# TensorE multiplies constants between the modulation groups, and loads go ahead of rotary stores

## The chip, the cores and the metric

The program runs on one core of one Trainium2 chip. The metric is the device time of one execution in microseconds (us); lower is better. The engines are TensorE (PE in the profile; PEld is its weight load), VectorE (DVE), ScalarE (ACT), GpSimd (POOL) and SyncE (SP), which here issues nearly all DMAs. SPq is the profile's name for SP's DMA queue.

## The reference

One step of a backbone with four layers over 256 context and 1024 latent tokens, model width 1024. Layers 0 and 3 mix tokens by multi-head latent attention (MLA), layer 1 by grouped-query attention, layer 2 by a banded one. Each layer is, cut to what matters here:

```python
sh, sc, gt = adaln(c, w_ada[i], b_ada[i])   # split(silu(c) @ w + b, 3)
h = rms_norm(x, norm_g[i]) * (1.0 + sc) + sh
z = h @ w_in                                # MLA: q, kv, rotary key, gate
q = rms_norm(cq, q_norm) @ w_uq             # 16 heads x (64 plain + 32 rotary)
kn, v = ckv_all @ w_ukv                     # keys and values of all tokens
o = softmax(q k^T) v
x = x + gt * ((o * silu(gate)) @ w_out[i])
```

The MLA layers rotate the 32 rotary features of each latent token's q by its grid position. Matrices are multiplied as pairs of float16 (a high part and a low part), three products each: high by high, high by low, low by high.

## The kernel before

Tokens lie along the free axis, features along the 128 partitions: `x_T` is 8 tiles of 128 features by 1280 tokens. Tokens go in three chunks of 512, 512 and 256 (`TOK_CHUNKS`). The program is a row of blocks, one after the other; all five engines meet between two blocks.

**The first block**, `start` (L176), makes the modulated input of layer 0. SP loads x, four small constants, then the modulation's weights in eight groups of 1.57 MB (`in_w_ada`, L238) into three slots: the load of group g, from 3 on, waits until TensorE has used up group g-3 (`s_row` has reached g-2). Behind group 5 go the first two weight tiles of the next block (`next_load`), behind group 7 the cache of layer 0. TensorE adds up the squares of x over partitions with a matrix of ones (L325, three float32 multiplications), then per group `group(g)` (L308, eight multiplications of a 32-column silu(c) with 384 weights each, float32), and `across(g)` (L296), which folds and transposes the row that VectorE has copied (`take_row`, L365). VectorE makes 1/rms by ScalarE's first value and Newton's three steps (L398 to L402), multiplies half of x by it (`times_rstd`, L369), and when groups 0 to 5 are through, finishes shift and scale (L413, L417; the second raises `s_fin`). From then on ScalarE and VectorE work through 24 parts n (chunk by feature tile): `product(n)` (L140), ScalarE's high part (L279 to L284), `low(n)` (L383, L385). `next_hi` and `next_low` (L780, L393) split the two weight tiles of the next block. `begin(t, c)` (L313, L320) is the first 2 x 2 tiles by chunks of the next block's product, 24 multiplications each, and waits part by part for `low`. At the end ScalarE and VectorE split the cache (L287, L437), SP stores four pieces of it (L245) and waits for them.

**The next block**, `project` (L801), starts with 48 multiplications of 256 columns that need nothing new, then with weights that SP loads at its start.

**The block `middle`** (L1301), once in layer 0 and once in layer 3, makes queries, keys and values in turns, one tile t a turn: 4 rotary tiles, 8 plain ones (turns 4 to 11), the first key tile (12), 14 value tiles, 7 more key tiles. Its weights come in pieces (`in_mla_uq`, `in_mla_uk`, `in_mla_uv`) through four landing buffers; the loads of turn t are split by ScalarE (L1490) and VectorE (L1542) at the start of turn t+2, and each may be issued when VectorE has split the piece that lay in its buffer, which it does at turn t. A tile's result is evicted by ScalarE (L1519) and VectorE (L1562); TensorE has three pairs of banks, so its unit u waits for the eviction of unit u-3. A tile has two units, of 1024 and of 256 columns (768 for a key tile). After turns 4 and 7 the rotated parts are stored: `turns_out = {4: 0, 7: 1}`, four stores of 8 heads x 16 rows x 1280 (L1409) each time, against four of 64 x 1280 for a plain tile (L1414). SP's order in a turn is: the turn's loads, its tile's stores, its rotary stores. Results lie in five slots (`wait_slot`), which the stores must have left before they are written again: the tile of turn 10 takes the slot of the first rotary part of turn 7, that of turn 11 the second's.

## Time and profile before

| | us |
|---|---|
| median of 3 runs | 4034.32 (4027.93 to 4036.26) |
| the profiled execution | 4037.71 |
| its span, first to last instruction | 4035.9 |
| TensorE busy with matmuls | 3893.6 (96% of the span) |
| VectorE, ScalarE, GpSimd busy | 2665.9, 2332.7, 1132.1 |
| mean granted TensorE clock | 0.988 |

The shares say that TensorE is the bound nearly everywhere. TensorE's clock has two levels, 1.2 and 2.4 GHz; the profile gives the granted level of a stretch as 0.50 or 1.00, and a stretch with both as a mean. Two parts of the program have something else in them: the first 80 us, where TensorE has little to do and waits, and the turns 8 to 12 of `middle`, around 285 to 320 us (layer 0) and 3167 to 3202 us (layer 3).

### The profile page before, as it was taken

The page shows a single profiled execution, that of the slowest core. Times are in us where ns is not written, and L with a number is a line of the kernel's source. Part 1 is how long each engine was busy: PE and PEld are TensorE (multiplying, and loading weights), DVE is VectorE, ACT ScalarE, POOL GpSimd, SP SyncE. Part 2 cuts the span into 40 slices and gives each one's busy share as a digit, 9 for nine tenths or more (in the row PEclk, how much of TensorE's full clock was granted, in tenths as well). Part 3 has the DMA queues.
Part 4 walks back from the last instruction along what each step waited for, and adds up shares of the span by engine and source line. Part 5 has one row for each costly group of instructions (what it writes and reads, how often), then busy time and mean ns, then how long its engine had stood idle before and what let it go on. Part 6 is the DMA issues. An engine that isn't in the chain of part 4 may idle for free. (4 is left out here: it accounts for less than half of the span.)

```text
span 4035.9 us, 57984 instructions
## 1 busy us (share of the span) xinstructions
PE 3893.6 (96%) x20892; PEld 1931.6 (48%) x20892; DVE 2665.9 (66%) x3536; ACT 2332.7 (58%) x3099; POOL 1132.1 (28%) x831
## 2 busy tenths in 40 slices
PE   6999999999999999999999999999999999999998
PEld 3554444444455544444445554555455444444444
DVE  6345777777457478888845427888543568777754
ACT  4433777777444358787843217888333457777762
POOL 0000343434230024454521003444210014444442
PEclk8999999999999999999999999999999999999999
DMA  6237323232102342222111324332111652212111
GB/s 241 65 102 223 92 55 77 60 72 64 60 32 76 116 113 51 65 64 62 37 66 51 108 91 117 91 90 63 62 46 70 186 151 46 55 42 55 42 38 66
DMA packets 376225, 329.42 MB, mean 82 GB/s; under 512 B 247664, under 2 KB 295344, under 8 KB 374480
## 3 DMA queue, kind: packets, MB, share of 16 engines
q1 hardware_dynamic: 376016, 326.60, 29.0%
q8 instruction: 135, 2.21, 0.2%
q14 instruction: 74, 0.61, 0.0%
HBM read 235.30 MB, written 91.23 MB: 81 GB/s over the span
## 5 line engine op out<-in xcount | busy, mean ns | idle before, releaser
L796 PE MATMUL bank<-H_hilo,w_hilo 128*128 128x512 f16 (+1 forms) x5760 | 1046.1, 344 | 13.6 <-DVE w_hilo L1046 10.1
L2238 ACT ACTIVATE p_f<-bank 128x1024 f32<-128x1024 f32 (+2 forms) x768 | 742.1, 966 | 485.9 <-PE bank L2184 454.6
L2184 PE MATMUL bank<-q_slots,k_slots 96*128 96x512 f16 (+7 forms) x3968 | 939.8, 366 | 6.0 <-PEq L1197 3.6
L1992 DVE TENSOR_REDUCE max_parts<-bank 128x1 f32<-128x512 f32 (+1 forms) x1248 | 799.1, 663 | 206.0 <-PE bank L1931 199.7
L2305 DVE TENSOR_TENSOR p_lo<-p_f,p_hi 128x1024 f16<-128x1024 f32 (+2 forms) x624 | 750.9, 1206 | 156.2 <-ACT p_hi L2242 151.6
L796 PEld LDWEIGHTS bank<-H_hilo,w_hilo 128*128 128x128 f16 x5760 | 563.7, 98 | 495.8 <-DVE w_hilo L1046 11.1
L2242 ACT ACTIVATE p_hi<-bank 128x1024 f16<-128x1024 f32 (+2 forms) x768 | 739.1, 962 | 0.0
L2184 PEld LDWEIGHTS bank<-q_slots,k_slots 96*128 96x128 f16 (+2 forms) x3968 | 369.7, 98 | 396.8 <-issue 27.0
L1931 PE MATMUL bank<-k_slots,q_slots 96*128 96x512 f16 (+4 forms) x1392 | 474.6, 369 | 24.9 <-DVE max_parts L1992 20.8
L2371 POOL TENSOR_TENSOR p_lo<-p_f,p_hi 128x1024 f16<-128x1024 f32 x144 | 315.6, 2192 | 567.5 <-ACT p_hi L2242 544.1
L2353 POOL TENSOR_TENSOR o_gated<-o_f,gate_rows 64x512 f32<-64x512 f32 (+1 forms) x192 | 235.5, 1226 | 778.5 <-DVE o_f L2285 571.5
L1010 ACT ACTIVATE z_ring<-bank 128x512 f32<-128x512 f32 (+1 forms) x192 | 87.5, 528 | 430.7 <-PE bank L796 417.2
L2151 PE MATMUL bank<-p_hi,cq_hilo 128*128 128x512 f16 (+1 forms) x832 | 308.5, 371 | 2.4 <-DVE p_lo L2305 1.8
L2155 PE MATMUL bank<-p_lo,cq_hilo 128*128 128x512 f16 (+1 forms) x832 | 307.9, 370 | 0.0
L2153 PE MATMUL bank<-p_hi,cq_hilo 128*128 128x512 f16 (+1 forms) x832 | 307.7, 370 | 0.0
L2151 PE MATMUL bank<-p_hi,v_hi_ones 128*128 128x512 f16 (+2 forms) x736 | 256.2, 350 | 21.9 <-DVE o_f L2285 14.9
L2153 PE MATMUL bank<-p_hi,v_lo_zeros 128*128 128x512 f16 (+2 forms) x736 | 257.3, 350 | 0.0
L2155 PE MATMUL bank<-p_lo,v_hi_ones 128*128 128x512 f16 (+2 forms) x736 | 255.8, 350 | 0.0
L1931 PEld LDWEIGHTS bank<-k_slots,q_slots 96*128 96x128 f16 (+1 forms) x1392 | 136.4, 98 | 231.2 <-DVE max_parts L1992 84.4
L1046 DVE SCALAR_TENSOR_TENSOR w_hilo<-w_f,w_hilo 128x1024 f16<-128x1024 f32 x56 | 68.6, 1224 | 258.8 <-ACT w_hilo L965 258.3
L2359 POOL TENSOR_TENSOR H_hilo<-o_gated,H_hilo 64x512 f16<-64x512 f32 (+3 forms) x192 | 218.0, 1136 | 22.9 <-POOL H_hilo L2357 13.3
L2357 POOL CAST H_hilo<-o_gated 64x512 f16<-64x512 f32 (+3 forms) x192 | 218.8, 1140 | 20.0 <-POOL o_gated L2353 12.3
(203 smaller groups left out, 3963.1 us busy)
## 6 DMA issues: line engine op xcount, KB each, us to landing
ada_w<-in_w_ada SPq DMA_DIRECT2D x48, 768.0 KB, 5.4
gate<-z_ring SPq DMA_DIRECT2D x32, 640.0 KB, 3.3
gate_rows<-gate SPq DMA_DIRECT2D x64, 320.0 KB, 4.0
q_slots<-q_mla SPq DMA_DIRECT2D x64, 240.0 KB, 3.2
k_mla<-H_hilo SPq DMA_DIRECT2D x64, 224.0 KB, 3.2
k_slots<-k_mla SPq DMA_DIRECT2D x64, 224.0 KB, 4.4
cq_hilo<-v_scratch SPq DMA_DIRECT2D x64, 224.0 KB, 3.3
w_f<-in_mla_in SPq DMA_DIRECT2D x24, 512.0 KB, 4.0
```

The source lines that it names most:

```text
L796: ins = pe.matmul(dst, lhs(a, k), rhs(b, k), start=(k == 0 and n == 0), stop=(k == nk - 1 and n == 2))
L1931: ins = pe.matmul(mb[:, 0:n], Q[0:kk, q_slot(hd, b), 0, q0:q0 + P], K[0:kk, k_slot(hd, b), 0, k0:k0 + n], start=True, stop=True)
L1992: dve.tensor_reduce(mx[:, par, t, c:c + 1], MB[(b * NE + k) % 2][:, 0:n], AX.X, ALU.max).then_inc(s_red.h, 1)
L2151: pe.matmul(d, V[:, b, kt], ph[:, slot[q], sel], start=first and n == 0, stop=False, skip_group_check=True)
L2153: pe.matmul(d, VL[:, b, kt], ph[:, slot[q], sel], start=False, stop=False, skip_group_check=True)
L2155: ins = pe.matmul(d, V[:, b, kt], pl[:, slot[q], sel], start=False, stop=fin, skip_group_check=True)
L2184: ins = pe.matmul(dst, lhs, rhs, start=(m == 0), stop=(m == len(ops) - 1), skip_group_check=swa)
L2238: act.activation(p32[:, p % 2, 0:cols], src, ACT.Exp, scale=scale).then_inc(s_p32.h, 1)
L2242: act.activation(ph[:, slot[p], 0:cols], src, ACT.Exp, scale=scale).then_inc(s_ph.h, 1)
L2305: dve.tensor_tensor(pl[:, slot[q], 0:cols], p32[:, q % 2, 0:cols], ph[:, slot[q], 0:cols], ALU.subtract).then_inc(s_pl.h, 1)
L2353: pool.tensor_tensor(og[rows, 0:nq], o32[rows, s, 0:nq], G[rows, q0:q0 + nq], ALU.mult).then_inc(s_og.h, 1)
L2371: pool.tensor_tensor(pl[:, slot[p], 0:cols], p32[:, p % 2, 0:cols], ph[:, slot[p], 0:cols], ALU.subtract).then_inc(s_pp.h, 1)
```

## The change

Three edits. In `start`, TensorE gets `keep_busy(n)`: n multiplications of a constant 128 x 128 float16 matrix with 512 columns of the constants, into a bank that a later product overwrites from its start. Ten stand ahead of group 0, five behind group 0, and five each behind groups 2 to 5 (behind the `across` that follows them, or ahead of the last one), and behind group 6. Group 0 moves ahead of the three sums of squares, group 7 into the middle of `begin(0, 0)`, `across(6)` behind it and `across(7)` behind `begin(1, 0)`. VectorE's two `next_low` go ahead of the finish of shift and scale, and its last two `take_row` move to n = 1 and n = 8. In `middle`, the rotary stores go from the end of turns 4 and 7 to turns 5 and 8, between the loads and the tile's stores.

```diff
+        busy, BUSY = self.c16[:, 0:4].rearrange("p j m -> p (j m)"), 5
+                def keep_busy(n):
+                    for _ in range(n):
+                        pe.matmul(flat[1][:, 0:4 * P], self.c16[:, 0], busy, start=True, stop=True)
+                def begin(t, c, k0=0, k1=KD):
+                    for k in range(k0, k1):
                 pe.wait_ge(s_in.h, s_in.base + 16 * len(consts))
+                pe.wait_ge(s_sc.h, s_sc.base + 2)
+                pe.wait_ge(s_c16.h, s_c16.base + 5)
+                keep_busy(2 * BUSY)
+                group(0)
+                keep_busy(BUSY)
                 pe.wait_ge(s_ss.h, s_ss.base + KD - 1)
...
+                for g in range(1, READY):
                     group(g)
-                    if g > 0:
-                        across(g - 1)
+                    across(g - 1)
+                    if g > 1:
+                        keep_busy(BUSY)
                 across(READY - 1)
-                for g in range(READY, KD):
-                    group(g)
+                group(READY)
+                keep_busy(BUSY)
                 pe.wait_ge(s_v.h, s_v.base + NC)
-                begin(0, 0)
-                for g in range(READY, KD):
-                    across(g)
+                begin(0, 0, 0, 5)
+                group(READY + 1)
+                across(READY)
+                begin(0, 0, 5, KD)
                 begin(1, 0)
+                across(READY + 1)
...
                 take_row(5)
+                next_low(0)
+                next_low(1)
...
-                next_low(0)
...
-                    if n == KD - 1:
-                        next_low(1)
-                    if n in (3, 7):
-                        take_row(READY + n // 4)
+                    if n in (1, KD):
+                        take_row(READY + n // KD)
...
+                    if t - 1 in turns_out:
+                        for item in (2 * turns_out[t - 1], 2 * turns_out[t - 1] + 1):
+                            sp.wait_ge(s_rl.h, s_rl.base + item + 1)
+                            store_item(sp, item)
                     if t in item_of:
                         sp.wait_ge(s_lo.h, s_lo.base + lows_of[t])
                         store_item(sp, item_of[t])
-                    if t in turns_out:
-                        for item in (2 * turns_out[t], 2 * turns_out[t] + 1):
-                            sp.wait_ge(s_rl.h, s_rl.base + item + 1)
-                            store_item(sp, item)
```

TensorE's program at the start of the first block, before:

```order
L325 MATMUL bank<-H_hilo,ones 128x512 x2
L325 MATMUL bank<-H_hilo,ones 128x256
L308 MATMUL bank<-ada_w,silu_c_wide 32x384 x16
L296 MATMUL bank<-fold_strips,ada_rows 128x2 x3
L308 MATMUL bank<-H_hilo,silu_c_wide 32x384 x8
```

And in the changed kernel:

```order
L317 MATMUL bank<-const_f 128x512 x10
L309 MATMUL bank<-ada_w,silu_c_wide 32x384 x8
L317 MATMUL bank<-const_f 128x512 x5
L336 MATMUL bank<-H_hilo,ones 128x512 x2
L336 MATMUL bank<-H_hilo,ones 128x256
L309 MATMUL bank<-ada_w,silu_c_wide 32x384 x8
L297 MATMUL bank<-fold_strips,ada_rows 128x2 x3
L309 MATMUL bank<-H_hilo,silu_c_wide 32x384 x8
L297 MATMUL bank<-fold_strips,ada_rows 128x2 x3
L317 MATMUL bank<-const_f 128x512 x5
```

The first group of weights now stands ahead of the sums of squares, with 15 multiplications of constants around it.

SP's DMAs of `middle` in turns 4 to 8, before (`w_f` is the landing buffer of the weights, `q_mla` the store of queries; the stores of 8x16x1280 are the rotary ones):

```order
L1414 DMA q_mla<-H_hilo 64x1280 x4
L1409 DMA q_mla<-H_hilo 8x16x1280 x4
L1442 DMA w_f_4<-in_mla_uq 128x384
L1442 DMA w_f_4<-in_mla_uv 128x2x128
L1414 DMA q_mla<-H_hilo 64x1280 x4
L1442 DMA w_f_4<-in_mla_uq 128x384
L1442 DMA w_f_4<-in_mla_uv 128x2x128
L1414 DMA q_mla<-H_hilo 64x1280 x4
L1442 DMA w_f_4<-in_mla_uk 128x256
L1442 DMA w_f_4<-in_mla_uv 128x2x128
L1414 DMA q_mla<-H_hilo 64x1280 x4
L1409 DMA q_mla<-H_hilo 8x16x1280 x4
```

And in the changed kernel:

```order
L1425 DMA q_mla<-H_hilo 64x1280 x4
L1453 DMA w_f_4<-in_mla_uq 128x384
L1453 DMA w_f_4<-in_mla_uv 128x2x128
L1420 DMA q_mla<-H_hilo 8x16x1280 x4
L1425 DMA q_mla<-H_hilo 64x1280 x4
L1453 DMA w_f_4<-in_mla_uq 128x384
L1453 DMA w_f_4<-in_mla_uv 128x2x128
L1425 DMA q_mla<-H_hilo 64x1280 x4
L1453 DMA w_f_4<-in_mla_uk 128x256
L1453 DMA w_f_4<-in_mla_uv 128x2x128
L1425 DMA q_mla<-H_hilo 64x1280 x4
```

The four rotary stores have moved behind two loads and stay ahead of the next tile's stores; it is the same again in turn 8 and in layer 3.

## Rows read from the trace of the kernel before

**Rows 1.** Busy time by stretch: start:end, length, busy (xinstructions) by engine, PEclk, DMA share, GB/s.
```profile
34.40:58.20 23.80, 20.03 (x107) 8.60 (x108) 16.84 (x23) 9.25 (x13) 0.00 (x0) 0.50 0.95 384
38.30:42.40 4.10, 4.10 (x23) 1.96 (x23) 3.36 (x3) 0.00 (x0) 0.00 (x0) 0.50 0.97 406
```

**Rows 2.** Timeline of the first block: start, length, engine, line, work [idle before <-releaser].
```profile
22.57 4.60 PE L325 MATMUL bank<-H_hilo,ones 128*128 128x512 f32 x6 [22.57 <-DVE H_hilo L358]
27.10 2.96 PE L308 MATMUL bank<-ada_w,silu_c_wide 128*32 128x384 f32 x32
...
39.60 2.79 PE L308 MATMUL bank<-ada_w,silu_c_wide 128*32 128x384 f32 x16
...
64.22 15.70 PE L320 MATMUL bank<-H_hilo,first_w_hilo 128*128 128x512 f16 x72
```

**Rows 3.** The same sum of squares in the next block, from TensorE's timeline.
```profile
129.25 2.31 PE L1142 MATMUL bank<-squares,ones 128*128 128x512 f32 x6
```

**Rows 4.** Busy time by stretch, as rows 1, where the DMA engines run dry, and after.
```profile
27.70:32.00 4.30, 4.30 (x54) 1.81 (x46) 2.42 (x3) 2.54 (x2) 0.00 (x0) 1.00 0.47 157
32.00:50.00 18.00, 14.70 (x82) 7.87 (x78) 11.11 (x13) 2.00 (x2) 0.00 (x0) 0.56 1.02 426
```

**Rows 5.** Timeline of VectorE, ScalarE and SP in the first block.
```profile
28.84 1.62 SPq L238 DMA_DIRECT2D ada_w<-in_w_ada  x2
...
30.61 1.48 DVE L398 TENSOR_TENSOR H_hilo<-rstd 128x1280 f32<-128x1280 f32 x1
...
46.70 2.00 ACT L780 ACTIVATE first_w_hilo<-next_w_f 128x1024 f16<-128x1024 f32 x2 [16.41 <-DMA next_w_f<-in_mla_in]
...
49.89 0.18 DVE L417 SCALAR_TENSOR_TENSOR ada<-ada,params 128x16 f32<-128x16 f32 x1
...
61.24 1.22 DVE L393 SCALAR_TENSOR_TENSOR first_w_hilo<-next_w_f,first_w_hilo 128x1024 f16<-128x1024 f32 x1
62.37 0.55 DVE L365 COPY ada_rows<-bank 128x384 f32<-128x384 f32 x1
...
64.40 0.72 ACT L284 ACTIVATE H_hilo<-xn,ada 128x512 f16<-128x512 f32 x1 [1.21 <-DVE xn L140]
...
74.38 1.05 ACT L287 ACTIVATE ckv_hilo<-ckv_f 128x1024 f16<-128x1024 f32 x1
```

**Rows 6.** TensorE's timeline at the start of the block project.
```profile
81.14 5.40 PE L796 MATMUL bank<-H_hilo,first_w_hilo 128*128 128x256 f16 x48 [1.22 <-PEq L226]
...
88.63 11.56 PE L796 MATMUL bank<-H_hilo,w_hilo 128*128 128x512 f16 x45 [2.08 <-DVE w_hilo L1046]
```

**Rows 7.** Busy time by stretch, as rows 1: project, and middle of layer 0.
```profile
89.00:92.30 3.30, 3.30 (x10) 1.18 (x8) 3.29 (x3) 1.79 (x3) 0.00 (x0) 0.50 0.83 304
314.30:317.60 3.30, 3.30 (x12) 1.46 (x10) 2.20 (x4) 1.32 (x3) 2.38 (x2) 0.50 0.82 256
```

**Rows 8.** Timeline of middle in layer 0, turns 4 to 11, all engines that matter there.
```profile
280.50 4.33 SPq L1409 DMA_DIRECT2D q_mla<-H_hilo  x4
283.64 0.55 DVE L1542 SCALAR_TENSOR_TENSOR w_hilo<-w_f,w_hilo 128x384 f16<-128x384 f32 x1
284.88 1.48 SPq L1442 DMA_DIRECT2D w_f<-in_mla_uq  x1
...
302.97 1.82 SPq L1442 DMA_DIRECT2D w_f<-in_mla_uk  x1
...
309.75 0.59 SPq L1442 DMA_DIRECT2D w_f<-in_mla_uk  x1
310.54 0.42 ACT L1490 ACTIVATE w_hilo<-w_f 128x256 f16<-128x256 f32 x1 [8.03 <-DMA w_f<-in_mla_uk]
...
312.89 0.42 ACT L1490 ACTIVATE w_hilo<-w_f 128x256 f16<-128x256 f32 x1 [0.35 <-DMA w_f<-in_mla_uk]
313.58 1.51 PE L796 MATMUL bank<-cq_hilo,w_hilo 128*128 128x256 f16 x9 [2.74 <-DVE H_hilo L1562]
```

**Rows 9.** The same wait of TensorE in layer 3.
```profile
3194.92 1.99 PE L796 MATMUL bank<-cq_hilo,w_hilo 128*128 128x256 f16 x9 [2.33 <-DVE H_hilo L1562]
```

More of the change, by code:

```diff
@@ L311, in group @@
                     ins.then_inc(s_row.h, 1)
-                def begin(t, c):
+                def keep_busy(n):
+                    for _ in range(n):
+                        pe.matmul(flat[1][:, 0:4 * P], self.c16[:, 0], busy, start=True, stop=True)
+                def begin(t, c, k0=0, k1=KD):
                     pe.wait_ge(s_nl.h, s_nl.base + t + 1)
                     t0, n = TOK_CHUNKS[c]
-                    for k in range(KD):
+                    for k in range(k0, k1):
                         pe.wait_ge(s_hl.h, s_hl.base + c * KD + k + 1)
@@ L325, in _ @@
                     pe.matmul(sums[c][:, 0:n], self.ones[:], ss[:, t0:t0 + n], start=True, stop=True).then_inc(s_sum.h, 1)
-                pe.wait_ge(s_sc.h, s_sc.base + 2)
-                pe.wait_ge(s_c16.h, s_c16.base + 5)
-                for g in range(READY):
+                for g in range(1, READY):
                     group(g)
-                    if g > 0:
-                        across(g - 1)
+                    across(g - 1)
+                    if g > 1:
+                        keep_busy(BUSY)
                 across(READY - 1)
-                for g in range(READY, KD):
-                    group(g)
+                group(READY)
+                keep_busy(BUSY)
                 pe.wait_ge(s_v.h, s_v.base + NC)
-                begin(0, 0)
-                for g in range(READY, KD):
-                    across(g)
+                begin(0, 0, 0, 5)
+                group(READY + 1)
+                across(READY)
+                begin(0, 0, 5, KD)
                 begin(1, 0)
+                across(READY + 1)
                 begin(0, 1)
```

## The prediction

> **What bounds the kernel now.** The page's first section shows TensorE busy for 96% of the span. So I looked for stretches where it waits for something that the change touches. Busy time by stretch shows two kinds: the first 80 us, with the clock at half from 34.4 to 58.2 [rows 1], and short half-clock stretches behind waits in project and in middle [rows 7]. The timelines then say what ends each wait.
>
> In the first block, shift and scale are ready at 50.07 (L417's end) [rows 5]; from there ScalarE and VectorE work through 24 parts until ScalarE turns to the cache at 74.38 [rows 5]. The next block begins 6.8 us later, with TensorE at 81.14 [rows 6]; TensorE itself had ended at 64.22 + 15.70 = 79.92 [rows 2]. So the end is set by the parts, the cache's split and its stores, and TensorE is 1.2 us early. Its half clock has cover here, and that is the first thing to hold against the bursts.
>
> What sets the 50.07? The two weight tiles of the next block land at 46.70 and are split behind it [rows 5]. They are late since the DMA engines run dry: 157 GB/s over the 4.3 us from 27.7, against 426 after 32.0 [rows 4]. That loses 4.3 x (1 - 157/426) = 2.7 us. Load 3 waits there for group 0, which stands behind the sums of squares; it is issued at 28.84 [rows 5].
>
> In middle, TensorE stands still for 2.74 us at 310.84, layer 3 for 2.33 [rows 8, 9], and its clock is at half after it, 3.3 us and more, worth another 1.7 [rows 7]. ScalarE had waited 8.03 us for a key weight that SP issued at 302.97, behind four rotary stores [rows 8].
>
> **The first block, step by step.** The ten multiplications wait for constants alone, which are there long before any group, and no data waits for them: they cost nothing. The DMA engines have delivered groups 0 to 2 at 27.7; a group of 1.57 MB takes 1.57/426 = 3.7 us, so group 0 is through at 20.3 and lands, with an estimated 1.2 for completion, at 21.5. Group 0 at half clock takes 2.79 [rows 2]. Five constants: a 512-column product at full clock takes 15.70/72 = 0.218 [rows 2], at half 0.44, so 2.2. The sums could have begun at 22.57 and now begin near 26.5. They took 4.60; the same sum takes 2.31 later, at full clock [rows 2, 3]. Between the two I take 2.7, since the clock comes to full some way into them: they end at 29.2 instead of 27.2, **+2.0** for 1/rms. Newton begins at 32.6 instead of 30.61 [rows 5].
>
> VectorE from there to the finish: three steps and four products by 1/rms at 1.48, four `take_row` at 0.55, both `next_low` at 1.22 [rows 5] = 10.4 + 2.2 + 2.4 = 15.0, so 47.6 at the earliest.
>
> The DMAs: load 3 is issued at 24.3 instead of 28.84 and closes the first part of the hole. Load 4 waits for group 1, now at 29.2 + 1.5 = 30.7, half of the pair that takes 2.96 [rows 2], and comes through some 0.9 us late. So 1.8 of the 2.7 are gained: the weight tiles are there at 44.9, ScalarE's two splits (2.00) end at 46.9, the second `next_low` at 48.1, the finish at 48.6: **-1.5**. The bursts behind groups 2 to 5 are 1.1 each at full clock, and group, `across` (an estimated 0.4; no row here has it alone) and burst are then 1.5 + 0.4 + 1.1 = 3.0 against 3.7 between landings: hidden. If the finish no longer waited for the weight tiles, the burst ahead of `across(5)` would show with its 1.1.
>
> Behind the finish one idle stretch of ScalarE goes: 1.21, ended by a product that stood behind `next_low(1)` and a `take_row` [rows 5]. **-1.2**. The two `take_row` stay, but VectorE now has no `next_low` of 1.22 behind its first products either, and this room takes them. TensorE needs 96 x 0.218 + 1.5 + 0.8 = 23.2 from about 51.0, so it ends at 74.2 or a little later, still ahead of the parts and the cache. The block ends at 81.1 - 2.7 = 78.4. Bounds: -4.6 (all 2.7 regained and sums as fast as before) to +1.2 (the clock never comes, below).
>
> **Project.** TensorE's wait ahead of its first product grows from 1.22 [rows 6] to some 3 us. Now its clock falls behind the second wait, of 2.08, and 3.3 us at half [rows 7] cost 1.7. If it falls before the first 48 products, they take up to 7.1 instead of 5.40, and end within the 7.5 us from 81.14 to 88.63 [rows 6]; then the second fall has no reason. Between 0 and -1.7 I take **-1.0**, nearer to the gain, since a wait of 2.08 was enough for a fall.
>
> **The bursts and the clock.** The stretch at 38.3 has TensorE busy for 4.10 of 4.10 us with groups and `across`, at 0.50 [rows 1]: these products did not bring the clock back. The page "TensorE: Matmul & The Clock Gate" of the Trainium skill (Part 1) says that activity releases the throttle, judged by how busy the engine is; by that rule alone the groups would have done it, and the bursts would be needless. The row disagrees. By the rule the block would come out as in my sum, since the bursts hide either way.
>
> **Middle.** Turn 8's loads now go ahead of the rotary stores and are there in time; but turn 5's loads also do, and they can't be issued before VectorE's splits of turn 5 at 283.64 and behind it [rows 8], since VectorE is busy with the rotary parts until then. The rotary stores were issued at 280.50, in that very wait [rows 8]. Now SP stands idle behind a blocked load from 280.5 to 284.1, and the stores start at 285.0 instead of 280.5. SP's 32 issues between 280.50 and 309.75, the first and last of its rows, stand without a gap over 0.3 us [rows 8], so the lag runs on: of 4.5 us, 1.2 is two loads already issued, and some 0.6 I take as slack. **2.7 us** stays at the loads of turn 9, behind both lots of rotary stores and turn 8's own. ScalarE gets them at 312.89 now [rows 8] and would at 315.6. These are its splits at the start of turn 11, behind which the eviction stands for which TensorE's second unit of turn 12 waits.
>
> TensorE's path: without the wait of 2.74 the unit of 313.58 starts at 310.0, the next at 310.9 and ends at 313.5; then TensorE waits for that eviction until 318.8. Before, it began this same unit at about 318.7, having lost 2.7 and 1.7 on the way. The gain of turn 10 is eaten whole. The clock then falls after a wait of 5.3, and costs up to 1.7 again: I take **+1.3** a layer, +2.6 for both. Bounds: -4.4 a layer (both waits gone, 2.7 and 1.7), +3.6 (the whole idle stretch of SP arrives).
>
> The page "DMA: Bandwidth & Descriptors" of the Trainium skill (Queues, rings and completion order) says that a DMA's data is spread over the largest number of engines up to 16 that divides its slowest dimension, which for 8 x 16 x 1280 would be 8 of 16. The trace has such a thing: the load behind these stores was being issued for 1.48 and 1.82 us, another for 0.59 [rows 8]. By the page the stores' slow drain moves with them and isn't shortened; my sum has it so.
>
> **Sum.** -2.7 - 1.0 + 2.6 = -1.1: the profiled execution of 4037.7 becomes 4036.6. The median of before is 3.4 below its profiled execution, so I forecast **4033.2**. A measurement of this kernel can tell about 0.2%, 8.1 us, from no change.
>
> **Rivals.**
> - *Middle's wait goes* (0.16). If turn 9's loads aren't late, because SP catches up by turn 7 as it does now, both layers give 4.4; with -3.6 at the start and -1.7 in project that is -14: 4020. For it: SP's issues of loads shrink to 0.59 when nothing clogs. Against: the 3.6 idle us of SP are certain by VectorE's row.
> - *The bursts don't bring the clock* (0.12). Group, `across` and burst at half take 2.8 + 0.7 + 2.2 = 5.7 against 3.7 per landing, and are the block's path: the finish comes near 52.5, +2.4; with -1.2 and middle's +2.6, +3.8: 4038. Against: full-width products brought the clock back in every other stage.
> - *Slower* (0.08). The lag of SP arrives whole: the rotary stores hold the slots of turns 10 and 11 until after 308 and 313, evictions wait for them, and TensorE loses 3.6 + 1.7 a layer beyond now; +10.6 - 2 = +8.6: 4043. It decides when VectorE's split of turn 5 comes more than 3 us after the stores could go, and nothing behind absorbs it.
> - *Nothing arrives* (0.14). The weight tiles land as late as before and TensorE's waits only move: 4034.
>
> My forecast has 0.50. The range leaves out most of the first rival and the far part of the third: 4023 to 4041. Chances: faster by over 0.2% (below 4026) 0.18; slower (above 4042) 0.08; within, 0.74.
>
> **What would show it.** The clock full from before 30 to the end of the first block; the DMA engines without a hole at 27.7; shift and scale at 48.6; the next block at 78.4. In middle: SP waiting ahead of the load of turn 5, ScalarE's long wait of turn 10 gone and one of 2 to 3 us at turn 11, TensorE's wait moved from 310.8 to 313 less 3.7. I'm wrong on middle if TensorE has no wait over 2 us there, and on the start if the block's end moves by less than 1 or over 5 us.

## The result, and the profile after

| | before | after |
|---|---|---|
| median | 4035.01 us (4027.93 to 4041.74, 20 runs) | 4040.59 us (4034.75 to 4048.26, 20 runs) |
| ratio, 95% interval | | 1.0014, 1.0008 to 1.002 |
| the profiled execution | 4037.71 us | 4036.22 us |

The kernel became 5.6 us slower. That is less than the 0.2% that the prediction took as the bound of its three cases, but the interval of this comparison lies wholly above 1, and the sign is not the forecast's. One run of the kernel before, of 4134.8 us at a mean clock of 0.942, is left out of all comparisons. The profiled execution of after is one of its faster ones and that of before one of its slower ones, so the two traces alone would tell a wrong story (-1.5 us). They are read here place by place, and sizes are taken from several traces.

The head of the page of after:

```profile
span 4034.4 us, 58064 instructions
PE 3896.1 (97%) x20932; PEld 1931.6 (48%) x20932; DVE 2668.0 (66%) x3536; ACT 2333.9 (58%) x3099; POOL 1135.4 (28%) x831
```

In `start`, first the timeline, then busy time by stretch (columns as in rows 1) over the stretch of [rows 4] in which the DMA engines had run dry, and over a later stretch:

```profile
21.39 2.79 PE L309 MATMUL bank<-ada_w,silu_c_wide 128*32 128x384 f32 x16 [7.96 <-DMA ada_w<-in_w_ada]
...
26.22 2.39 PE L336 MATMUL bank<-H_hilo,ones 128*128 128x512 f32 x6
...
43.99 2.00 ACT L791 ACTIVATE first_w_hilo<-next_w_f 128x1024 f16<-128x1024 f32 x2 [12.11 <-DMA next_w_f<-in_mla_in]
...
47.57 0.17 DVE L431 SCALAR_TENSOR_TENSOR ada<-ada,params 128x16 f32<-128x16 f32 x1
```

```profile
27.70:32.00 4.30, 4.30 (x42) 1.85 (x40) 0.65 (x2) 4.00 (x5) 0.00 (x0) 1.00 0.98 409
46.90:53.60 6.70, 5.90 (x24) 1.78 (x25) 6.37 (x12) 4.97 (x8) 0.00 (x0) 0.50 0.99 373
```

The hole in the DMA stream is closed (409 GB/s for 157), the weight tiles are there at 43.99 instead of 46.70 [rows 5], and shift and scale are ready at 47.74 instead of 50.07. Project, from TensorE's timeline, answers to [rows 6]:

```profile
77.12 5.40 PE L807 MATMUL bank<-H_hilo,first_w_hilo 128*128 128x256 f16 x48 [0.34 <-PEq L227]
85.75 14.44 PE L807 MATMUL bank<-H_hilo,w_hilo 128*128 128x512 f16 x78 [3.23 <-DVE w_hilo L1057]
```

It begins 4.0 us earlier, but after its first 48 products TensorE waits 3.23 us for 2.08, so that only 2.9 are left at 85.75.

Middle of layer 0, timeline of SP, ScalarE and TensorE, answers to [rows 8]. The whole stands 4.6 us earlier here:

```profile
273.43 2.47 SPq L1425 DMA_DIRECT2D q_mla<-H_hilo  x4
279.66 0.34 SPq L1453 DMA_DIRECT2D w_f<-in_mla_uq  x1
280.05 0.60 SPq L1453 DMA_DIRECT2D w_f<-in_mla_uv  x1
280.69 4.37 SPq L1420 DMA_DIRECT2D q_mla<-H_hilo  x4
...
298.64 12.57 PE L807 MATMUL bank<-cq_hilo,w_hilo 128*128 128x256 f16 x63 [2.30 <-DVE H_hilo L1573]
...
306.90 1.30 ACT L1530 ACTIVATE H_hilo<-bank 128x1024 f16<-128x1024 f32 x2 [4.16 <-DMA q_mla<-H_hilo]
...
312.71 0.42 ACT L1501 ACTIVATE w_hilo<-w_f 128x256 f16<-128x256 f32 x1 [4.51 <-DMA w_f<-in_mla_uk]
...
315.79 3.36 PE L807 MATMUL bank<-ckv_hilo,w_hilo 128*128 128x512 f16 x12 [1.98 <-DVE H_hilo L1573]
```

SP has issued a tile's stores at 275.90 and then stands idle to 279.66, where VectorE frees a landing buffer (it ends a split at 279.63). Only then come the rotary stores. In the kernel before they filled just this gap [rows 8]. The one wait of TensorE of 2.74 us [rows 8] has become two, of 2.30 and 1.98, and each has a stretch of 3.4 us at half clock behind it (299.44 to 302.85 and 316.50 to 319.92 in the clock's record), where before had one. In layer 3 the one wait of 2.33 us [rows 9] has become three, but the clock falls once, as before (3190.52 to 3193.94):

```profile
3177.51 9.91 PE L807 MATMUL bank<-cq_hilo,w_hilo 128*128 128x256 f16 x54 [1.03 <-DVE H_hilo L1573]
3189.37 1.16 PE L807 MATMUL bank<-cq_hilo,w_hilo 128*128 128x256 f16 x9 [1.95 <-DVE H_hilo L1573]
...
3196.61 2.12 PE L807 MATMUL bank<-ckv_hilo,w_hilo 128*128 128x512 f16 x12 [1.80 <-DVE H_hilo L1573]
```

### The profile page after: what moved, and what is told of

Same layout as the page of the kernel before. It is cut to its first block and busy times, and to the rows that moved or that the text cites. A ratio compares the mean times of both kernels' runs of the same rounds, so it can differ in the third digit from the quotient of the medians.

```text
span 4034.4 us, 58064 instructions
## 1 busy us (share of the span) xinstructions
PE 3896.1 (97%) x20932; PEld 1931.6 (48%) x20932; DVE 2668.0 (66%) x3536; ACT 2333.9 (58%) x3099; POOL 1135.4 (28%) x831
```

## How the sizes are taken

All kernels of this study end in the same matmuls. So the n-th matmul from the end of a trace can be set against the n-th from the end of the trace of before: the difference of their starts is how late (+) or early (-) TensorE is there. This table, worked out so, holds one profiled execution each. "Start and project" is the difference at the end of project, "middle" what it grows by over the block; between the two and behind layer 3 the kernels are the same, and that part scatters by some us from one execution to the next. `start_only` and the other names are the experiments below.

```
                    start+project  middle, layer 0  middle, layer 3    end
before, as timed         0.00            -                -             0.00
middle_only             -1.66          +3.12            +3.28          +4.91
turn8_only              -1.45          -2.22            -0.06          -4.17
turn5_only              +0.29          +3.55            +6.17          +9.54
six_before              -1.65          -3.82            -2.74          -6.45
after                   -4.56          +3.19            +3.38          -1.47
start_only              -3.12          +0.18            +0.70          -6.70
start_turn8             -1.77          -1.14            -0.38          -5.77
six_after               -2.27          +1.47            +1.19          +1.90
start_thin_burst        -2.48          -1.93            +1.56          -6.73
start_no_burst          -6.05          -0.03            +0.39          -4.66
after_no_burst          -4.20          +2.80            +3.49          -1.02
six_start_no_burst      -5.77          -3.65            -0.20         -11.98
six_turn8_no_burst      -3.98          -2.69            -0.19         -11.42
```

The trace of before has one of the slower first blocks: the five executions that have the old block `start` stand at 0, -1.66, -1.45, +0.29 and -1.65, mean -0.9. The five that have the new one with its added products (after, start_only, start_turn8, six_after, start_thin_burst) have a mean of -2.8. The change's 4.6 us at this point are thus nearer to 2 in the mean.

The times, with the mean and its standard error. Medians are compared with runs of the kernel before on the same chip, which gives the ratio. Differences of means in the text are taken from 4035.4, the mean of before over four sets of runs (4035.2, 4035.0, 4035.7 and 4035.7), so that the choice of set moves them by up to 0.4:

| kernel | median us (range, runs) | mean | ratio, 95% interval |
|---|---|---|---|
| before, all four sets | 4035.2 (4027.9 to 4042.0, 115) | 4035.4 +/- 0.2 | |
| after | 4040.59 (4034.75 to 4048.26, 20) | 4041.2 +/- 0.8 | 1.0014 (1.0008 to 1.002) |
| start_only | 4035.46 (4028.09 to 4039.89, 11) | 4034.6 +/- 1.1 | 1.0 (0.9991 to 1.0009) |
| middle_only | 4043.36 (4041.4 to 4046.07, 11) | 4044.0 +/- 0.6 | 1.0021 (1.0012 to 1.003) |
| turn8_only | 4033.63 (4028.71 to 4035.81, 11) | 4033.1 +/- 0.6 | 0.9995 (0.9986 to 1.0004) |
| start_turn8 | 4035.18 (4027.46 to 4039.34, 11) | 4034.7 +/- 1.0 | 0.9999 (0.999 to 1.0008) |
| turn5_only | 4044.24 (4038.53 to 4047.24, 11) | 4043.7 +/- 0.8 | 1.0019 (1.001 to 1.0028) |
| six_after | 4039.61 (4033.38 to 4044.69, 11) | 4038.4 +/- 1.2 | 1.0009 (1.0 to 1.0018) |
| six_before | 4030.58 (4027.92 to 4034.53, 11) | 4030.7 +/- 0.6 | 0.9987 (0.9978 to 0.9996) |
| start_no_burst | 4030.28 (4026.67 to 4036.31, 11) | 4030.6 +/- 0.9 | 0.9988 (0.9979 to 0.9997) |
| start_thin_burst | 4033.93 (4028.78 to 4038.04, 11) | 4033.7 +/- 0.9 | 0.9994 (0.9985 to 1.0003) |
| after_no_burst | 4038.42 (4036.01 to 4041.02, 11) | 4038.5 +/- 0.5 | 1.0007 (0.9998 to 1.0016) |
| six_start_no_burst | 4026.69 (4023.07 to 4028.88, 8) | 4026.1 +/- 0.8 | 0.9976 (0.9965 to 0.9986) |
| six_turn8_no_burst | 4026.88 (4024.64 to 4030.53, 11) | 4027.4 +/- 0.5 | 0.9981 (0.9972 to 0.999) |

## Experiments: the change in halves

**start_only** is after with the order of stores in `middle` put back:

```diff
-                    if t - 1 in turns_out:
-                        for item in (2 * turns_out[t - 1], 2 * turns_out[t - 1] + 1):
-                            ...
                     if t in item_of:
                         ...
+                    if t in turns_out:
+                        for item in (2 * turns_out[t], 2 * turns_out[t] + 1):
+                            ...
```

> The changed kernel with middle's rotary stores put back to the end of turns 4 and 7. Theory A (the first block gives 4.6 us and keeps it, middle's new order takes over 3 us a layer): 4.6 us faster than before, about 4030, with TensorE level with the changed kernel up to middle and 3 us ahead of it behind middle of layer 0. Theory B (the bursts or the first block's new order cost something later, the stores' place doesn't matter): no faster than before, 4036 to 4041, TensorE's lead of 4.6 us lost somewhere else than in middle.

**middle_only** is the kernel before with that edit alone, the other way round.

> The kernel before with the rotary stores moved to turns 5 and 8, the first block untouched. Theory A: 3.2 us more in each of the two middles, 6 to 7 us slower, about 4041; TensorE's wait of 2.74 us in turn 11 gone and new ones in turns 8 to 9 and 12. Theory B: within 1 us of before, 4035.

Measured: the start's edits alone give a mean of 4034.6, which can't be told from before; the middle's alone 4044.0, +8.6. So the whole loss comes from moving eight stores per layer, and the start brings next to nothing. In middle_only's trace the two middles cost 3.1 and 3.3 us, the same as in after. That is 6.4 of the 8.6; where the rest lies is not shown. Of the theories, A is right on the stores; the 4.6 us that it gave to the start did not arrive, as B had said.

## Experiments: which of the two moves in middle

Both lots of rotary stores moved by a turn. **turn8_only** moves only the later lot, from turn 7 to turn 8:

```diff
+                    if t - 1 in turns_out and turns_out[t - 1] in (1,):
+                        ...the two rotary items, as in the change
                     if t in item_of:
                         ...
-                    if t in turns_out:
+                    if t in turns_out and turns_out[t] not in (1,):
```

> The kernel before with only the second lot of rotary stores (turn 7) moved behind the loads of turn 8; the first lot stays at the end of turn 4. Theory A (SP stood idle ahead of turn 5's blocked loads, and that lag is what costs): no idle time of SP at turn 5, loads of turn 8 there in time, TensorE's wait of 2.74 us and the half clock behind it smaller or gone, 0 to 3 us a layer faster than before, about 4032. A rival to A (the drain of the rotary stores costs wherever they stand, because turn 10 needs their slot back): slower than before by 2 us a layer or more, with ScalarE waiting for the stores of queries in turn 10.

**turn5_only** has (0,) in place of (1,): the earlier lot goes from turn 4 to turn 5, the later stays.

> The kernel before with only the first lot of rotary stores (turn 4) moved behind the loads of turn 5. Theory A (SP idles behind turn 5's blocked loads and everything on its queue comes late from there): the whole loss of middle_only and some more, since turn 8's loads still stand behind the second lot: 7 to 10 us slower than before, about 4044, with about 4 us of SP's idle time at turn 5 and ScalarE's wait for turn 8's loads longer than the 8.03 us of before. Rival (the second lot and its slots cost): within 1 us of before.

**start_turn8** is start_only with the later lot moved.

> The changed kernel's first block with only the second lot of rotary stores moved. Theory A: the sum of start_only and turn8_only, 5 to 10 us faster than before, 4025 to 4030. Theory B: no faster than before.

Measured: turn5_only costs 8.3 (4043.7), as much as both moves. turn8_only has a mean 2.3 lower (4033.1; 1.9 against the runs on its own chip), but the interval of its ratio includes no change; on top of the start's edits the same move gives nothing (4034.7 and 4034.6), so the sum that theory A expected of start_turn8 failed. The timeline of turn5_only, SP, ScalarE, and TensorE:

```profile
278.28 2.48 SPq L1414 DMA_DIRECT2D q_mla<-H_hilo  x4
284.51 0.34 SPq L1442 DMA_DIRECT2D w_f<-in_mla_uq  x1
284.90 0.60 SPq L1442 DMA_DIRECT2D w_f<-in_mla_uv  x1
285.54 4.34 SPq L1409 DMA_DIRECT2D q_mla<-H_hilo  x4
...
295.33 0.59 SPq L1442 DMA_DIRECT2D w_f<-in_mla_uq  x1
...
302.05 9.91 PE L796 MATMUL bank<-cq_hilo,w_hilo 128*128 128x256 f16 x54 [0.85 <-DVE H_hilo L1566]
...
314.18 0.42 ACT L1494 ACTIVATE w_hilo<-w_f 128x256 f16<-128x256 f32 x1 [9.96 <-DMA w_f<-in_mla_uk]
...
317.20 2.10 PE L796 MATMUL bank<-cq_hilo,w_hilo 128*128 128x256 f16 x9 [5.25 <-DVE H_hilo L1566]
```

The gap from 280.76 to 284.51 is empty; the rotary stores start 5.0 us later than in [rows 8], of which 0.3 is the whole trace's. The load at 295.33, turn 6's, stands at 290.79 in the trace of before: 4.5 less 0.3 = 4.2 late, one turn after the move. Turn 8's (307.16 for 302.97) is 3.9 late and turn 9's (313.49 for 309.75) 3.4. ScalarE's long wait of 8.03 [rows 8] has grown to 9.96 and TensorE's of 2.74 to 5.25, with another of 0.85. 5.25 + 0.85 - 2.74 = 3.4 of the 3.55 us that this middle costs. SP's queue has hardly a gap in between and gives back 0.8 of the 4.2 us in three turns: it is the queue that paces these turns. In layer 3 the same move costs 6.17, with waits of 1.33 and 6.23 us for one of 2.33, and one execution doesn't tell whether that is typical.

turn8_only shows what the other move does:

```profile
305.75 1.30 ACT L1523 ACTIVATE H_hilo<-bank 128x1024 f16<-128x1024 f32 x2 [4.07 <-DMA q_mla<-H_hilo]
...
314.36 2.12 PE L796 MATMUL bank<-ckv_hilo,w_hilo 128*128 128x512 f16 x12 [1.39 <-DVE H_hilo L1566]
```

Turn 10's key weight is now early (split at 300.97, 310.54 before), but ScalarE waits 4.07 us for a store to leave a slot of `H_hilo`, and TensorE still waits 1.39. Loads and stores of one queue trade places, and what goes behind is late. This wait of 1.39 us has no half-clock stretch behind it, and layer 0 comes out 2.2 us shorter; in layer 3 nothing is gained.

## Experiments: more landing buffers

If the queue paces the turns because a load may only be issued when its buffer is free, then more buffers let SP run ahead. **six_after** and **six_before** have six landing buffers for four in `middle`, the two new ones in an unused tail of `H_hilo`, on the order of stores of after and of before:

```diff
-        SLOTS, DEPTH_W, LANDING, BATCH = 5, 4, 4, 5
+        SLOTS, DEPTH_W, LANDING, BATCH = 5, 4, 6, 5
-        wf = sb("w_f32", [P, LANDING, QK_, P], F32)
+        own_wf = sb("w_f32", [P, 4, QK_, P], F32)
+        spare = self.H[:].rearrange("p s k n -> p (s k n)")[:, SLOTS * 2 * KEYS:].bitcast(F32)
+        lands = [own_wf[:, b] for b in range(4)] + [...two pieces of spare...]
```

> The changed kernel with six landing buffers for middle's weights instead of four (two in the unused tail of the tile H_hilo), so that each load is issued three turns ahead of its split instead of two; the order of stores is that of the changed kernel. Theory A (late loads): TensorE's waits of 2.30 us (turn 9) and 1.98 us (turn 12) go, 3 to 7 us a layer faster than the changed kernel, about 4030. Rival S (the slots that rotary stores hold make ScalarE wait in turns 7 and 10, and that is what TensorE waits for): waits for stores stay and it is no more than 2 us faster than the changed kernel, about 4039.

> The kernel before with six landing buffers. Theory A: ScalarE's wait of 8.03 us in turn 10 goes, with TensorE's 2.74 us and the half clock behind it: 3 to 4.4 us a layer, 6 to 9 us faster than before, about 4027. Rival S: no faster than before.

Measured: -4.7 on the order of before (4030.7), -2.8 +/- 1.4 on that of after (4038.4). six_before's TensorE has no wait of note between 284 and 321:

```profile
284.07 26.10 PE L796 MATMUL bank<-cq_hilo,w_hilo 128*128 128x256 f16 x144 [0.68 <-DVE H_hilo L1565]
```

The wait of 2.74 and the half clock behind it are gone, -3.8 us in layer 0 and -4.2 up to the end of middle's turns in layer 3 (-4.71 at 3166, -8.89 at 3203 in the table's terms; 1.5 of them are given back behind it). In six_after ScalarE waits elsewhere:

```profile
309.46 1.30 ACT L1533 ACTIVATE H_hilo<-bank 128x1024 f16<-128x1024 f32 x2 [7.59 <-DMA q_mla<-H_hilo]
...
311.80 1.66 PE L807 MATMUL bank<-cq_hilo,w_hilo 128*128 128x256 f16 x9 [3.16 <-DVE H_hilo L1576]
```

With the loads early, the late stores themselves hold the slots: 7.59 us for ScalarE and 3.16 for TensorE, as rival S had it for this order; on the order of before, theory A holds. So the lag that the move at turn 5 starts seems to show at whichever of the two, loads or slots, runs out first. Of the two orders with six buffers, the difference is 7.7 us (4038.4 and 4030.7), with the start's edits on the slower side.

## Experiments: what the bursts cost

**start_no_burst** is start_only with an empty `keep_busy`; all other edits of the start, group 0 ahead of the sums among them, stay:

```diff
-                    for _ in range(n):
+                    for _ in range(0):
```

> start_only without the multiplications of constants: the first block's new order alone. Theory C (the bursts pay): the clock is at half from the sums or soon after until the first product, shift and scale come 1 to 3 us later than in start_only, 1 to 2 us slower than it. Theory D (the bursts only move instruction loading into the next block's first weight loads, and these lose 1.2 us there): the next block's first weights land 4.2 us after their issue instead of 5.4, and the whole is level with start_only or up to 1.5 us faster, 4033.

Measured: a mean of 4030.6, against 4034.6 with the bursts and 4035.4 before. The bursts cost 3.9 +/- 1.4 us, and that is most of the 4.8 that the rest of the start's edits gain; theory D had the direction and at most 1.5 us. Its timeline, and busy time by stretch:

```profile
47.24 0.17 DVE L431 SCALAR_TENSOR_TENSOR ada<-ada,params 128x16 f32<-128x16 f32 x1
...
76.78 5.40 PE L807 MATMUL bank<-H_hilo,first_w_hilo 128*128 128x256 f16 x48 [1.26 <-PEq L227]
84.27 15.95 PE L807 MATMUL bank<-H_hilo,w_hilo 128*128 128x512 f16 x85 [2.08 <-DVE w_hilo L1057]
```

```profile
27.00:41.40 14.40, 8.95 (x92) 4.63 (x88) 11.89 (x11) 2.90 (x3) 0.00 (x0) 1.00 1.01 420
41.60:51.70 10.10, 8.94 (x48) 4.00 (x38) 7.22 (x12) 5.41 (x8) 0.00 (x0) 0.50 1.01 400
```

The clock is full from 24.5 to 41.5 without a burst, and falls later; with the bursts it falls too, from 46.85 to 53.68 (the second stretch of after above). The finish is at 47.41 with no burst and 47.74 with them. So at the finish the bursts bring nothing: the clock there is hidden in the new order, as the DMA stream paces the groups at 420 GB/s. What they cost stands in project. Without them TensorE resumes at 84.27, with them at 85.75. The DMA view of 77 to 83 us, of after (the GB/s are those of 40 slices of 0.15 us):

```profile
GB/s 0 0 0 0 0 0 0 218 191 82 191 355 273 218 137 300 300 355 355 519 382 382 410 410 355 437 382 382 191 27 55 27 27 27 27 27 27 0 27 0
q8 instruction: 1, 0.02, 1.0%
w_f<-in_mla_in SPq DMA_DIRECT2D x2, 512.0 KB, 5.4
```

and of start_no_burst, from 76 to 82, so that it holds the same two loads:

```profile
GB/s 0 0 0 0 0 0 0 0 0 0 0 218 82 137 246 273 328 218 218 355 355 328 410 437 437 437 437 437 437 437 300 219 109 55 55 27 0 0 0 0
q1 hardware_dynamic: 288, 1.05, 51.1%
w_f<-in_mla_in SPq DMA_DIRECT2D x2, 512.0 KB, 4.2
```

The row of q8 is a block of instructions that is loaded by DMA. After has 136 of them in all, before and start_no_burst 135. In after the third falls between 78 and 81 us, right behind the first loads of project; in start_no_burst it comes between 84 and 87, and in before one comes between 63 and 66, the next between 90 and 93. The first two weight loads of project, issued in the same 3 us, land after 5.4 us (median of the two) instead of 4.2, which is also what they take in the trace of before. The slices show how: in after the stream stops at 81.4 but for some 27 GB/s, which is one packet of 4 KB per slice, until 82.9, where in start_no_burst it fades out over some five slices.

That could be the number of instructions, or what the wide products do. **start_thin_burst** keeps all 40 products and their 40 weight loads, but 8 columns wide:

```diff
-                        pe.matmul(flat[1][:, 0:4 * P], self.c16[:, 0], busy, start=True, stop=True)
+                        pe.matmul(flat[1][:, 0:8], self.c16[:, 0], busy[:, 0:8], start=True, stop=True)
```

> The start's edits with all 40 products of the bursts left as instructions, but 8 columns wide in place of 512, so that they keep TensorE busy for next to nothing. The full bursts gave a mean of 4034.6, no bursts 4030.6. Theory L, the added instructions cost (a block of code is loaded behind them, into project's first weight loads): the finish stays as it is, project resumes near 85.7 with a wait over 3 us in place of 84.27 with 2.08, a row of q8 stands in the first 6 us of project, and the mean is 4032 to 4035. Theory C, the bursts' work costs (it moves the stretches at half clock, which then fall into project): the resume stands at 84.3, no q8 row there, and the mean is 4030 to 4032. If both cost, the resume is 85.7, no stretch at half clock lies in project and the mean is 4032 to 4033.

Measured: a mean of 4033.7, 3.0 +/- 1.2 above no bursts and not to be told from the full ones. Project in its timeline, and the DMA view of 77 to 83:

```profile
86.14 14.06 PE L807 MATMUL bank<-H_hilo,w_hilo 128*128 128x512 f16 x65 [3.88 <-DVE w_hilo L1057]
```

```profile
q8 instruction: 1, 0.02, 1.0%
w_f<-in_mla_in SPq DMA_DIRECT2D x2, 512.0 KB, 5.3
```

The late resume and the row of q8 are there with products that keep TensorE busy for next to nothing: it is the instructions that cost; whether their work costs besides is not excluded (0.9 +/- 1.4 us between the two). Over all 14 traces the split is clean. The five with added products have a q8 row in the first 6 us of project, a median of 5.3 to 5.5 us for the first two loads, and a resume at 85.6 to 86.4. The nine without have no such row, a median of 4.1 to 4.4 us, and, of these, the four with the new start resume at 84.3 to 84.7. That is 1.5 us in the mean. In all 14 TensorE resumes 2.47 us after the second load has landed, so it is this landing that sets the resume. The page "Runtime: NRT & Kernel Launch" of the Trainium skill (Instruction fetch mechanics) says that instructions come in blocks of 256 by the sequencer's own DMA queue, ahead of their use and mostly hidden; the blocks are there in the trace, 0.02 MB each, and hidden they were not. How the block delays the weights can be seen in part. Its packet takes 0.96 us (1.0% of 16 engines' 6 us). The two loads are 256 packets of 4 KB, 16 for each of the 16 DMA engines if they are spread evenly. In all five traces with the q8 row the last eight or nine of them end one at a time, 1.1 to 1.9 us behind all others; in the nine without, at most three do. That fits one engine that was held up while the other 15 were not. The trace doesn't say which engine took which packet, so that it was the one with the block is inferred. The rest of what the bursts cost is partly clock: the longer wait was followed by a half-clock stretch in four of the five traces with added products, and in two of four without. One such stretch of start_only, by busy time:

```profile
85.50:88.80 3.30, 3.16 (x8) 1.17 (x9) 3.27 (x4) 2.14 (x4) 0.00 (x0) 0.50 0.86 315
```

Four and two of a handful are too few to price that part. At the end of project the traces with added products stand at a mean of -2.8 and the four without at -5.0, so 2.2 us of the 3 to 4 are found there, 1.5 of them at the resume. That another number of products would place the block elsewhere and cost nothing was not tried.

**after_no_burst** is the whole change with an empty `keep_busy`.

> The whole change without the products of the bursts. If the parts add up: the change's 4040.6 less the 3.9 that lie between the start's edits with and without bursts (means 4034.6 and 4030.6) gives 4036.7, still slower than the kernel before (4035.0) or level with it, with TensorE's waits of some 2.3 and 2.0 us at turns 9 and 12 of the middle and a resume of project near 84.3. If the order of the stores only costs this much because the start is early, or if the bursts cost it nothing, it stays at 4040.

Measured: 4038.5, 2.7 +/- 1.0 below after, 3.1 above before. The resume is at 84.42, TensorE's waits in middle are 0.59, 1.48 and 3.33 us, middle costs 2.8 and 3.5. The two causes stand apart: the bursts cost 2.7 +/- 1.0 and 3.9 +/- 1.4 us with the two orders of the stores, the order 7.8 +/- 1.0 without the bursts and 6.6 +/- 1.4 with them.

## Experiments: what is left when both are undone

**six_start_no_burst** joins the start's edits without bursts, the old order of the stores, and six landing buffers.

> The start's edits without bursts, the stores of the middle in the order of the kernel before, and six landing buffers in place of four. Theory A, the two gains lie at different places and add up: -4.4 and -4.3 from 4035.0 give 4026.3, range 4024 to 4029, TensorE without a wait over 1 us between 280 and 313, project resumed near 84.3. Theory R, whatever the start gives is lost again at the middle's loads (the rival in which the middle is bound by when its queue gets on): 4030 to 4031, as either alone.

**six_turn8_no_burst** moves the later rotary lot besides.

> As the one before it, and only the rotary stores of turn 7 are issued in turn 8, behind its loads; those of turn 4 stay. With four landing buffers that move gave -1.9 (means 4033.1 and 4035.0), by sending the two loads of turn 9 ahead of four stores. With six these loads are early anyway, so theory A gives the same time as without it, 4026 +/- 1.5. Theory S, four stores later mean slots of H_hilo that come free later: ScalarE then waits on a store of q_mla for 3 to 7 us before turns 10 or 11, as it did for 4.1 with that move alone, TensorE for 1 to 3, per layer, and the time is 4028 to 4032.

Measured: 4026.1 (ratio 0.9976, 0.9965 to 0.9986), 9.3 us better than before and 15.1 than after. The two gains, 4.8 and 4.7 by the means, add up. TensorE's timeline in middle of layer 0, and in layer 3 behind it:

```profile
279.95 26.10 PE L807 MATMUL bank<-cq_hilo,w_hilo 128*128 128x256 f16 x144 [0.68 <-DVE H_hilo L1576]
```

```profile
3204.93 0.28 PE L1945 MATMUL bank<-k_slots,q_slots 96*128 96x256 f16 x1 [1.98 <-DMA k_slots<-kpe_mla]
```

No wait is left in the turns. In layer 3 the time gained there (4.2 us) comes back as 3.8 right behind it: the first scores wait 1.98 us for a key load, and the clock falls behind that wait (half from 3205.9 to 3209.3). That is what is late next. The later lot's move brings nothing more (4027.4 against 4026.1): its loads are early anyway, and ScalarE waits 3.89 and 2.09 us on slots instead, behind which TensorE does not stand still in the turns.

## Why the prediction was wrong, point by point

**The finish of shift and scale** was put at 48.6 and came at 47.74. The hole in the DMA stream closed as worked out, the weight tiles were there at 43.99 (44.9 forecast), the sums cost 1.3 us rather than 2.0, since their six products ran at half clock for 0.15 us only. The mechanism was right; by these two traces it was too small by 0.9, but that was partly luck of the base. The five executions with the old start finish at 48.26 to 50.18, mean 49.1, those with the new one at 47.4 to 47.7: 1.5 in the mean, as forecast. Two terms of the sum had no row of their own. `across` was put at 0.4 and takes 0.83 at full clock, which stays hidden; the 1.2 us for completion is shown by no run, but group 0's products began at 21.39, where 21.5 was said.

**The block's end** was put at 78.4 and came at 77.12: the finish's 2.3 and 1.7 from there to ScalarE's cache (24.31 us before, 22.60 now), where 1.2 was said for its idle stretch, which is gone. Right in kind; but the gain was counted from a trace whose own first block was late. Five traces with the old start begin project at 81.14, 79.35, 79.70, 81.27 and 79.59, mean 80.2, those with the new one between 76.8 and 77.1. The typical gain at this point is 3.2, not 4.0.

The scatter of the old block goes with the clock, which the prediction left out. In the two late executions (before and turn5_only) the clock is at half from 34.3 to 58.3 without a break, and the finish comes 3.4 us after the weight tiles; in the three early ones it is full from 46.5 or 46.7 on for 3.4 us, and the finish comes 2.2 us after the tiles. So in the old order the half clock seems to have shown at the finish, by 1.1 us, in two executions of five.

**"They cost nothing"**, of the bursts, was the first step that failed. They are hidden where they stand, as the sum said. They cost behind the block, in project, by 40 products and 40 weight loads more in the instruction stream. And the gain for which they would stand, the clock, came without them. What I had read from [rows 1], that groups and `across` do not bring the clock back from half, does not hold beyond that trace. In middle_only, which has the same block, it went back to full at 46.45 with nothing but these products on TensorE since 39.62, and so it did in turn8_only, six_before and after_no_burst:

```profile
39.70:46.40 6.70, 4.75 (x27) 2.12 (x24) 1.99 (x3) 0.39 (x1) 0.00 (x0) 0.50 1.02 426
46.50:49.80 3.30, 1.39 (x16) 1.31 (x20) 2.29 (x6) 2.17 (x4) 0.00 (x0) 1.00 1.02 428
```

And in start_no_burst they held it at full from 27.0 to 41.4, busy for 8.95 of 14.40 us, so that there was little to bring back. The rule of the page "TensorE: Matmul & The Clock Gate" of the Trainium skill (Part 1), that activity releases the throttle, fits these stretches and not the one in [rows 1].

**Project** was put at -1.0 for a half-clock stretch that should go. In after's trace it is gone, worth 1.7, and a wait longer by 1.2 us took part of that back: from 4.0 at project's start to 4.6 at its end, -0.5 where -1.0 was said. In the four other traces with added products the stretch is not gone. In the mean project gives back 1.3 us (3.2 at its start, 1.9 at its end): the term has the wrong sign. The four traces without added products gain 3.2 and 4.1, so -0.9, nearly what was said. It is the bursts' instructions that turned the term.

**Middle**, +1.3 a layer, is the term that decides, and it was +3.2 and +3.4. The mechanism was the right one: SP idle behind the blocked load (280.5 to 284.1 forecast, 280.76 to 284.51 in turn5_only), the rotary stores behind it, a late key weight at turn 11, TensorE's wait there. Two things failed. The first was the slack: of SP's 4.5 us I let 1.8 be absorbed, 1.2 by the order and "some 0.6 as slack", and kept 2.7 for turn 9's loads. ScalarE's split at turn 11 came at 312.71 + 4.56 = 317.3 on before's scale, not 315.6: 4.4 us late. The queue gave back next to nothing. The second was to follow the lag to one place. The same lag hits the splits of turn 8 and the slots of turn 10 on its way, and TensorE stops at 296.3 for 2.30 us as well as at 313.8 for 1.98. Layer 0, with a half-clock stretch behind each stop: waits 2.30 + 1.98 - 2.74 = +1.5; one more stretch at half clock, +1.7; together +3.2, what the table has. Layer 3, with as many such stretches as before: waits 1.03 + 1.95 + 1.80 - 2.33 = +2.45, of +2.6 in the turns, and 0.8 behind them. "The lag arrives whole" was in the prediction, as a rival with 0.08, priced at 5.3 a layer and 4043. Its mechanism is the one that came, at some 3.3 a layer. That the time still lies near 4043 is in part luck: middle_only is at 4044.0 and turn5_only at 4043.7, so that the later move gives nothing back, and after lies 2.8 +/- 1.0 below middle_only with the start's edits.

**The sum** with the terms as measured: -1.8 at the resume of project (mean of the five traces with added products, 85.9, less that of the five with the old start, 87.7), +6.6 in the two middles: +4.8, against 5.6 measured. The forecast of -1.1 fell by two steps: the lag of SP in middle, +1.3 a layer for +3.3, and the bursts put at nothing.

## What to carry to other kernels

An in-order issue queue with no gap in it is a resource like an engine. Before an entry is moved behind a wait, look at what the queue did in that wait: if the entry used to fill it, as here, nearly the whole wait is added to what is behind, and it can show at each place where a buffer or a slot is short, with a clock fall behind it or not. Slack along such a queue has to be read from a gap in its rows, not granted.

Instructions added to keep an engine's clock up can cost by their code even when their run time is hidden, as the 8-column products show: look where the next block of instructions is loaded, and what transfer is urgent there. And where the first block's trace is the base of a sum, one execution is too few: the same code began project anywhere from 79.35 to 81.27.

## What the runs showed of the hardware that was not expected

- 80 more TensorE instructions moved an instruction load of 0.02 MB from 84 to 87 us to 78 to 81, to the start of project, and with it two weight loads of 0.5 MB took 5.3 to 5.5 us (median) instead of 4.1 to 4.4, in five traces of five; their last eight or nine packets of 4 KB ended one by one.
- TensorE's clock held its full level over 14.4 us in which TensorE was busy for 8.95, with products of float32 and no burst (start_no_burst), and for some 17 us in the two kernels with six buffers that have the same start; in the trace of before the same kind of products, busy for 4.10 of 4.10 us, ran at the half level [rows 1]. In four other executions these products alone were on TensorE when the clock went back to full (at 46.45 in middle_only).
- A wait of TensorE of 2 us could be followed by a half-clock stretch of 3.4 us, as at 298.6 and 315.8 in after, which makes it worth 3.7 us and not 2. Not each was: waits of 2.38 us (start_turn8, layer 0), 2.09 (start_thin_burst, layer 0) and 3.23 (after, in project) had none behind them.
